# Scan steps of a hybrid block: the input strip ahead of the state products, the convolution stage behind them

## What is computed

```python
p = rms_norm(h) @ w_in                        # 4096 columns: 12 blocks of 128 for Hyena, 20 for HGRN2
# Hyena: short convolution (3 taps) of 12 blocks, then twice: z = gate * fft_long_conv(z)
# HGRN2: 4 heads, forward and backward, in chunks of time:
scores = (q * exp(b - b_mid)) @ (k * exp(b_mid - b)).T      # masked, per chunk
S_next = exp(b_last) * S + (k * exp(b_last - b)).T @ v      # state, from chunk to chunk
o = scores @ v + (q * exp(b)) @ S
o = o * rsqrt(mean(o * o)) * norm_w * silu(g)
h = h + concat(rms_norm(y_hyena), o) @ w_out
```

## Time and profile before

| | |
|---|---|
| median of 3 runs | 2412.01 us (2411.89 to 2413.15) |
| profiled execution: its own time | 2412.75 us |
| profiled execution: its span in the trace | 2411.0 us |
| PE busy, share of the span | 2049.6 us, 85% |
| DVE busy | 898.8 us, 37% |
| ACT busy | 283.0 us, 12% |
| scan, first scores to last output products | 193.8 to 288.7 us of the span |

### The profile page before, as it was taken

How to read it: one execution, slowest core, us unless ns; L and a number is a source line. 1 busy time by engine, 2 the same in 40 slices (tenths; PEclk the granted TensorE clock), 3 DMA queues, 4 the chain that set the end, 5 groups by cost and what they waited for, 6 DMA issues and landing times. The chain is left out here.

```text
span 2411.0 us, 24360 instructions
## 1 busy us (share of the span) xinstructions
PE 2049.6 (85%) x10160; PEld 1368.2 (57%) x10160; DVE 898.8 (37%) x1489; ACT 283.0 (12%) x636; POOL 0.2 (0%) x4
## 2 busy tenths in 40 slices
PE   7999987676766666666667999999999999999998
PEld 5466763332322222222223887788885877788887
DVE  5355631221211111111113364465553244465553
ACT  1101210000000000000002222210002212111001
POOL 0000000000000000000000000000000000000000
PEclk9999988888898888888788999999999999999999
DMA  6111069999999999999996243334444333234442
GB/s 232 70 70 70 10 292 422 428 428 427 428 427 428 428 429 428 429 428 429 429 428 269 90 164 113 131 105 157 157 174 142 132 140 140 105 114 144 147 154 88
DMA packets 45194, 592.32 MB, mean 246 GB/s; under 512 B 5463, under 2 KB 6904, under 8 KB 7800
## 3 DMA queue, kind: packets, MB, share of 16 engines
q1 hardware_dynamic: 43672, 585.43, 60.2%
q10 hardware_dynamic: 1440, 5.70, 0.6%
HBM read 590.07 MB, written 1.05 MB: 245 GB/s over the span
## 5 line engine op out<-in xcount | busy, mean ns | idle before, releaser
L510 PE MATMUL ps<-arena,ring 128*128 128x256 f32 x1856 | 413.8, 378 | 0.1
L510 PEld LDWEIGHTS ps<-arena,ring 128*128 128x128 f32 x1856 | 345.7, 189 | 50.6 <-issue 2.9
L1550 PE MATMUL ps<-ring,arena 128*32 128x512 f32 x2048 | 257.2, 649 | 92.6 <-DMA ring<-in_w_experts 73.2
L723 PE MATMUL ps<-arena,ring 128*128 128x256 f32 x1280 | 289.2, 378 | 0.0
L1577 PE MATMUL ps<-ring,arena 128*32 128x512 f32 x1024 | 172.7, 808 | 114.3 <-DMA ring<-in_w_experts 108.1
L723 PEld LDWEIGHTS ps<-arena,ring 128*128 128x128 f32 x1280 | 241.5, 189 | 35.6 <-issue 1.0
L1550 PEld LDWEIGHTS ps<-ring,arena 128*32 128x32 f32 x2048 | 64.0, 115 | 265.6 <-issue 142.3
L1577 PEld LDWEIGHTS ps<-ring,arena 128*32 128x32 f32 x1024 | 32.8, 129 | 238.3 <-DMA ring<-in_w_experts 160.3
L729 PE MATMUL ps<-arena,ring 128*128 128x256 f32 x640 | 151.8, 379 | 0.3 <-DVE arena L954 0.2
L1537 PE MATMUL ps<-arena 128*128 128x128 f32 x512 | 89.9, 358 | 67.2 <-DVE arena L2076 67.2
L1168 DVE RECIPROCAL arena<-arena 128x256 f32<-128x256 f32 x80 | 140.3, 1754 | 2.7
(11 more groups left out here) (372 smaller groups left out, 1832.9 us busy)
## 6 DMA issues: line engine op xcount, KB each, us to landing
ring<-in_w_experts SPq DMA_DIRECT2D x192, 2048.0 KB, 25.5
ring<-in_w_layers SPq DMA_DIRECT2D x42, 2048.0 KB, 7.8
ring<-in_w_layers SPq DMA_DIRECT2D x40, 1536.0 KB, 6.5
ring<-in_w_first SPq DMA_DIRECT2D x10, 2048.0 KB, 8.4
arena<-in_w_mem SPq DMA_DIRECT2D x2, 2048.0 KB, 28.8
arena<-in_mem ACTq DMA_DIRECT2D x2, 1024.0 KB, 7.0
arena<-in_fourier SPq DMA_DIRECT2D x1, 1632.0 KB, 20.7
arena<-in_gm_rows ACTq DMA_DIRECT2D x2, 768.0 KB, 4.9
```

Source lines behind the costliest of these rows:

```text
L510: last = pe.matmul(ps[:, j % 2, 0:SEQ], t[:, s, k, :], lhs[:, k, :], start=(k == 0), stop=(k == KD - 1))
L723: last = pe.matmul(ps[:, j % 2, 0:SEQ], t[:, k, :], an[:, k, :], start=(k == 0), stop=(k == KD - 1))
L1550: last = pe.matmul(ps[CAP * e:CAP * (e + 1), v // 4, :], xg[:, (v % 4) * 2 + k, CAP * e:CAP * (e + 1)], w[:, k, e, :], start=(v % 4 == 0 a ...
```

## The change

In steps 0 to 4 and in step 6 the two fillers are exchanged: the strip stands between the transposed keys and the state products, the convolution stage between the state products and the output products. This holds for PE, ACT and DVE alike, since all three read the same table. On ACT the factors of heads 0 and 1 are moved ahead of `between(6, 0)`, because strip 30 now stands there, and the squares of the Hyena result are moved behind `between(6, 1)`. No instruction is added or removed.

```diff
-BETWEEN = (("conv", 8), ("strip", 25), ("conv", 9), ("strip", 26), ("conv", 10), ("strip", 27), ("conv", 11), ("strip", 28),
-           ("conv", 12), ("strip", 29), ("conv", 13), ("conv", 14), ("conv", 15), ("strip", 30), ("strip", 31), ("", 0))
+BETWEEN = (("strip", 25), ("conv", 8), ("strip", 26), ("conv", 9), ("strip", 27), ("conv", 10), ("strip", 28), ("conv", 11),
+           ("strip", 29), ("conv", 12), ("conv", 13), ("conv", 14), ("strip", 30), ("conv", 15), ("strip", 31), ("", 0))
...
                 act.copy(xr(kd_t[0:CHH]), ps[0:CHH, 7, 0:(NCH - 1) * P]).then_inc(sem("keys_t"), 1)
+                if it == 6:
+                    act.wait_ge(sem("ss_head"), 2)
+                    head_rstd(0)
+                    head_rstd(1)
                 between(it, 0)
                 if it < 2 * NH - 1:
                     scan_exp(it + 1)
                 if it in (2, 4, 6):
                     head_squares(it // 2 - 1)
+                between(it, 1)
                 if it == 6:
-                    act.wait_ge(sem("ss_head"), 2)
-                    head_rstd(0)
-                    head_rstd(1)
                     act.wait_ge(sem("z"), 12)
                     act.activation(hyena_sq, conv[:, 0:4, META:T], ACT.Square).then_inc(sem("sq_hy"), 1)
-                between(it, 1)
```

## The result

| | before | after |
|---|---|---|
| median | 2411.99 us (2411.14 to 2413.69, 6 runs) | 2421.62 us (2418.45 to 2424.43, 6 runs) |
| ratio | 1 | 1.0038, 95% interval 1.0026 to 1.0051 |
| profiled execution: span | 2411.0 us | 2420.2 us |

The change costs 9.6 us. The forecast was 2414.8 with a range up to 2418.5, and slower by over 0.2% had a chance of 0.13: the prediction was wrong.

A forecast was written before the change was run, and what follows sets the result against it. The experts' weight stream, then PE, bound the kernel, and a late scan delays both. Pauses summed to +3.3 us, less 0.5 for the clock: +2.8 on 2412.01, thus 2414.8 us, range 2411.8 to 2418.5.

The forecast's parts named there:

- What bounds the steps, and the ceiling: Scan steps: PE waits for the state on DVE; removing the waits of steps 1 to 3 gains at most 3.6 us.
- Chain and cover: Each scan step: ACT and DVE time from strip to state (3.9 or 5.3 us) against PE work left, giving PE's wait.
- sum at unchanged clock: Scan steps: +1.9 (step 0), -3.6 (steps 1 to 3), +1.4 (step 4), +2.2 and +1.4 (step 6), together +3.3 us.
- What is moved past in each queue: ACT and DVE queues: delayed `scan_exp` costs nothing; DVE's 3.84 us of stage work hides beside 6.0 us of PE work.
- The clock term: Half speed in steps 3 and 6: the first kept, the second covered by a wait, taking 0.5 us off, to +2.8.
- one of three pauses drew a fall: Steps 1 to 3: of three equal pauses one was followed by a clock fall; used against expecting more falls.
- the fall at step 6: Half speed across the start of step 6, stage 15 at 3.50 instead of 3.11; covered by strip 30's wait, saving 0.5.
- about 0: Rival's further case: the clock falls of steps 3 and 6 both go, net change about 0; the rival had chance 0.20.
- The carry to the end: From the scan through routing to the experts' stream: a scan delay reaches the end one for one.
- hardly a byte: The eight scan steps, 193.8 to 288.7 us: said to move hardly a byte, unlike the experts' 422 to 429 GB/s.
- more falls of the clock: Rival: half speed in strips of steps 1, 5, 7 and stage 9; two falls give +5.4 to +6.2 us; chance 0.13.

The follow-up runs named there:

- step 6 alone: The kernel before with the exchange in step 6 only, the head factors moved ahead of it on ACT: 2417.55 us, ratio 1.0023.

## Why the prediction was wrong

With two profiles of each kernel, the means differ by 9.2 us of span, and divide so: pauses 10.51 against 7.58, +2.9; busy 106.8 against 102.6, which is the clock, +4.2 (1.8 to 6.6 by which profiles are paired); up to the first scores +1.0; from L1495 to the end +1.1.

- **What bounds the steps, and the ceiling** were right. The three pauses of the earlier trace rows went.
- **Chain and cover** was right, within 0.3 us at each place. Forecast 1.9, 1.4, 2.4 and 1.4 us of new pauses at four places; measured 1.67, 1.45, 2.20 and 1.45 at those places. The sum at unchanged clock was +3.3; the pauses rose by 2.6 to 3.3.
- **What is moved past in each queue** was right for the full change: `scan_exp` behind the strip's copy costs nothing. DVE's six instructions behind `scan_inputs` are hidden by a strip only; in the kernels where a stage followed they cost 1.35 and 1.47.
- **The clock term failed.** The forecast kept the number of falls, put one of them over the wait of step 6, and took 0.5 us off. Measured: half clock of 17.1 and 20.4 us against 13.7 and 6.8, and +4.2 us instead of -0.5. Four errors are in it. First, one profile was read as the state of the kernel: both falls inside its steps are missing in the second profile, so the base to which pauses were added was better than it looked. Second, the fall behind step 7's pause of 2.3 us was not weighed. It stands in 9 of the 9 profiles that leave that pause empty, and in one of the four that fill it. Third, the rule "one of three pauses drew a fall" was taken over to longer pauses. Over all profiles the 1.1 us pauses of steps 1 to 3, where left empty, were followed by half clock within 3 us in 2 of 16 cases; the new ones of steps 0 and 4 (1.67 and 1.45) in 8 of 8, the last one of step 6 (1.45) in 3 of 3. Where products fill these long ones it is 0 of 4. Length alone doesn't decide it, though: the 2.20 us ahead of strip 30 was followed by no fall in both profiles of the changed kernel (step 6 alone was at half clock already), nor were the 1.35 and 1.47 us ahead of stages 12 and 11, in 3 of 3; the 0.85 us ahead of strip 30 was in 2 of 7. In the 11 of 11 small output products, scores and keys follow the pause; behind the others a strip or a stage follows at once. Which of the two matters, length or what follows, is not separated by these runs. Fourth, a fall was priced too low. Stage 11 at half clock was set against stage 9 (7.18 - 5.90 = 1.3), but stage 11 itself takes 5.63 at full clock in the second profile, which makes 1.55. And of the fall at step 6 only what fell on stage 15 was counted, 0.5, though it began at 264.5 and covered head sums, scores and keys too; 3.4 us at half clock at 0.46 are 1.6. So "about 0" for both falls gone doesn't follow from the prediction's own terms either, which give +1.5. The half clock ahead of strip 30 that was expected to be hidden wasn't there in either profile of the changed kernel.
- **The carry to the end** was taken one for one and holds within the scatter. From L1495 to the end the thirteen profiles have 2105.1 to 2108.0 us, the changed kernel 2108.0 and 2105.1, before 2105.7 and 2105.2. The load of the experts that the earlier trace rows tells of left at 301.52 us before and leaves 6.9 later now, exactly as much as L1495 is later (312.22 against 305.31). That the scan moves "hardly a byte" was read too broadly, has 305 GB/s in step 3; the step doesn't rest on it.

```profile
308.43 2.56 SPq L1286 DMA_DIRECT2D ring<-in_w_experts  x4
```

- **The rival that came true** is the first, more falls of the clock, with its mechanism and its places: the half clock is in steps 1, 5 and 7. It had a chance of 0.13 and a price of 5.4 to 6.2 for two falls. The stretch rose by 7.2 on the mean of the profiles, and the time by 9.6 and 8.5, above the upper end of this rival as well. The rule of the Trainium skill that spoke against the change (page "TensorE: Matmul & The Clock Gate", section "A second HAM failure mode: psum-queue depth-cycling": frequent small pauses make the clock swing) fits what happened at the pauses of steps 0, 4, 6 and 7, and not at those of 2.20, 1.35 and 1.47 us, so the traces agree with it in part.

What stays open are the 1.0 us ahead of the first scores and the 1.1 behind L1495. The first is most likely scatter: first scores start at 193.7 to 194.9 in nine profiles and at 195.5 to 196.1 in four, those four have twice as long at half clock in the first 25 us (a granted clock of 0.86 or 0.87 against 0.93), and they include the fastest kernel. Before and after, over the first 25 us:

```profile
0.00:25.00 25.00, 12.17 (x36) 8.46 (x36) 5.71 (x16) 6.32 (x7) 0.20 (x4) 0.93 0.94 349
```

```profile
0.00:25.00 25.00, 11.93 (x29) 8.62 (x30) 5.71 (x16) 5.93 (x6) 0.20 (x4) 0.86 0.95 343
```

The second lies within what code that is equal in this part shows, 2.9 us. That neither belongs to the change is argued from two profiles of each kernel, not shown.

## What to carry to other kernels

When an order is changed, compare for each step the chain behind the moved piece with the work that is left to cover it; here that gave every new pause of the change within 0.3 us, and missed the wait of a stage for DVE's work on the stage before in the two kernels where the exchange stops at step 2 or 3. Then price the pause twice, once as its length and once as the clock it draws down. Here the clock was the larger part (3.4 us for the change with the pauses filled in both kernels, 8.5 and 9.6 without), and a second profile of the unchanged kernel would have shown that its own stretches at half clock come and go. Where a pause can't be removed, products that nobody reads, fitted into it, can pay: they took about 7 us from the changed kernel, and with the exchange kept to steps 1 to 3 they gave 2406.53, 5.0 below the unchanged kernel beside it.

## What the runs showed of the hardware

- A microsecond at half clock cost 0.46 us on this mix of matmuls, by the busy times of two profiles; eleven others fit it within 0.6 us of 104 to 118.
- Pauses far shorter than the stretches at half clock that followed them were enough for TensorE to fall to 1.2 GHz: ahead of the small output products it did so after 1.1 us in 2 of 16 cases, after 1.45 and 1.67 in 11 of 11, and after 1.45 and 1.67 filled with unused products in 0 of 4. Ahead of a strip or a stage it did not after 2.20 (2 cases) or after 1.35 and 1.47 (3 cases), and did after 0.85 in 2 of 7.
- Two profiles had a fall with no pause in the 20 us ahead of it, behind step 5.
- In the first 25 us, before anything differs between the kernels, the length at half clock differs from execution to execution (granted clock 0.93 in nine profiles, 0.86 or 0.87 in four), and the four have their first scores 1 to 2 us later than most.
